# Query and key heads normed and rotated with tokens on partitions instead of features, in a two-block f32 kernel on one core

## What is computed

```python
def rms_norm(x, g):
    y = xf * lax.rsqrt(jnp.mean(xf * xf, axis=-1, keepdims=True) + EPS)
    return (y * g.astype(jnp.float32)).astype(x.dtype)

def apply_axial_rope(x, cos, sin):            # features as (2, 2, 32)
    xs = x.reshape(x.shape[:3] + (2, 2, HEAD_DIM // 4))
    x1, x2 = xs[..., 0, :], xs[..., 1, :]
    out = jnp.stack([x1 * c - x2 * s, x2 * c + x1 * s], axis=-2)
    return out.reshape(x.shape)
...
    bg_l, cg_l, vc_l, q_l, k_l, v_l, gt_l = jnp.split(hx @ w_in[layer], SPLITS, axis=-1)
    y_conv_l = conv_branch(bg_l, cg_l, vc_l, conv_w[layer])
    q = rms_norm(q.reshape(B, L, N_Q_HEADS, HEAD_DIM), q_g)   # split_heads
    k = rms_norm(k.reshape(B, L, N_KV_HEADS, HEAD_DIM), k_g)
    q_l = apply_axial_rope(q_l, cos, sin)
    k_l = apply_axial_rope(k_l, cos, sin)
    k_all = jnp.concatenate([k_c, k_l], axis=1)
    o_l = latent_attention(q_l, k_all, v_all)
```

## Time and profile before

| what | value |
|---|---|
| median of 3 runs | 1324.51 us (1324.28 to 1335.15) |
| the profiled execution, its own time | 1324.45 us |
| its span in the profile | 1322.6 us |
| PE busy | 1304.7 us, 99% of the span |
| DVE, ACT, POOL busy | 903.0 us (68%), 644.3 us (49%), 27.3 us (2%) |
| instructions | 23508 |
| HBM read | 227.63 MB |
| granted TensorE clock | full in all of the 40 slices |

### The profile page before, as it was taken

The page is one execution under the profiler, slowest core; times in us unless marked ns, Lnnn a source line. Parts: engine busy times, 40 slices in busy tenths (PEclk is TensorE's granted clock), DMA queues, the critical chain, the costliest instruction groups (busy, mean ns, idle before and its releaser), DMA issues. The chain is left out here.

```text
span 1322.6 us, 23508 instructions
## 1 busy us (share of the span) xinstructions
PE 1304.7 (99%) x9348; PEld 1210.0 (91%) x9348; DVE 903.0 (68%) x1455; ACT 644.3 (49%) x1027; POOL 27.3 (2%) x27
## 2 busy tenths in 40 slices
PE   9999999999999999999999999999999999999998
PEld 6788888888889999999999999989999999999998
DVE  4768775555658587554775555788887665689873
ACT  4622311222236345554555445666665765556552
POOL 0000000000010000000000000200000000100000
PEclk9999999999999999999999999999999999999999
DMA  9755555646635354545556665556546455436760
GB/s 358 270 186 191 191 191 192 222 159 215 204 107 161 111 159 130 159 128 160 178 155 194 190 201 174 171 159 184 148 143 181 128 174 176 145 112 208 217 197 33
DMA packets 201485, 230.20 MB, mean 174 GB/s; under 512 B 7073, under 2 KB 191649, under 8 KB 201377
## 3 DMA queue, kind: packets, MB, share of 16 engines
q1 hardware_dynamic: 201088, 228.42, 54.7%
q10 hardware_dynamic: 288, 0.28, 0.1%
HBM read 227.63 MB, written 1.05 MB: 173 GB/s over the span
## 5 line engine op out<-in xcount | busy, mean ns | idle before, releaser
L1105 PE MATMUL P<-XHB,WH 128*128 128x256 f32 (+1 forms) x1808 | 553.1, 306 | 7.4 <-DVE XLB L1784 3.9
L1106 PE MATMUL P<-XLB,WH 128*128 128x256 f32 (+1 forms) x1808 | 543.2, 300 | 0.0
L1107 PE MATMUL P<-XHB,WL 128*128 128x256 f32 (+1 forms) x1808 | 543.2, 300 | 0.0
L1988 DVE TENSOR_TENSOR WL<-W,WH 128x1024 fp32r<-128x1024 f32 x358 | 431.7, 1224 | 87.2 <-ACT WH L1565 87.0
L1565 ACT ACTIVATE WH<-W 128x1024 fp32r<-128x1024 f32 x358 | 369.0, 1042 | 249.3 <-PE P L1107 157.8
L1105 PEld LDWEIGHTS P<-XHB,WH 128*128 128x128 f32 x1808 | 340.0, 188 | 27.7 <-issue 8.2
L1106 PEld LDWEIGHTS P<-XLB,WH 128*128 128x128 f32 x1808 | 340.1, 188 | 15.2 <-issue 0.5
L1107 PEld LDWEIGHTS P<-XHB,WL 128*128 128x128 f32 x1808 | 340.2, 188 | 14.6
L1105 PE MATMUL P<-GH,WH 128*128 128x256 f32 (+1 forms) x372 | 121.2, 326 | 0.0
L1106 PE MATMUL P<-GL,WH 128*128 128x256 f32 (+1 forms) x372 | 120.6, 324 | 0.0
L1107 PE MATMUL P<-GH,WL 128*128 128x256 f32 (+1 forms) x372 | 120.6, 324 | 0.0
(11 more groups left out here) (322 smaller groups left out, 1797.3 us busy)
## 6 DMA issues: line engine op xcount, KB each, us to landing
W<-in_ffn_w_in SPq DMA_DIRECT2D x88, 512.0 KB, 4.8
W<-in_w_in_ab SPq DMA_DIRECT2D x72, 512.0 KB, 4.6
W<-in_w_modt SPq DMA_DIRECT2D x56, 512.0 KB, 3.9
W<-in_w_in SPq DMA_DIRECT2D x52, 512.0 KB, 4.1
W<-in_ffn_w_out SPq DMA_DIRECT2D x40, 512.0 KB, 4.8
W<-in_w_in_c SPq DMA_DIRECT2D x32, 512.0 KB, 4.3
W<-in_w_out_ab SPq DMA_DIRECT2D x16, 512.0 KB, 4.4
W<-in_w_out_c SPq DMA_DIRECT2D x16, 512.0 KB, 4.7
```

The lines of the kernel that those rows point to most:

```text
L1105: pe.matmul(o, h[:, k, c], xh[:, kk, a:b], start=kk == 0, stop=False)
L1106: pe.matmul(o, h[:, k, c], xl[:, kk, a:b], start=False, stop=False)
L1107: mm = pe.matmul(o, l[:, k, c], xh[:, kk, a:b], start=False, stop=kk == gm.nk - 1)
L1988: dve.tensor_tensor(l, a, h.bitcast(F32), ALU.subtract).then_inc(S["wl"], 1)
```

## The change

Queries and keys are now produced with tokens on partitions: the q and k gemms run unturned. k is then 96 matmuls of 256 columns in place of 48 of 512, and `K` and `Q` first hold tokens by features. Its second chunk is walked tile by tile. The unit of work of `qk_norm` is one gemm: two heads of q for 256 tokens, that is four blocks of 128 tokens by 128 features (u = 0 to 3), or k with eight blocks (u = 4). Each unit has three kinds of steps:

- `qs` (ACT, lines 1619 and 1623): each block is squared with a running sum over its row (`accum_out`), and one root is taken over 128x4 or 128x8 values.
- `qr` (DVE): one reciprocal of the same small size (2142); per block a scalar-tensor-tensor with the sine table on the swapped halves (2156) and one with the cosine table (2162), each of which multiplies also by the token's root; two additions of 128x256 (2167). The context blocks of k take one scalar-tensor-tensor each, by the gain (2153).
- `qt`: four PE transposes of 128x128 (1201), into one bank, and one ACT copy of 128x512 back to `Q` or `K` (1628, 1632). k has two such steps. PE waits there for all of the unit's DVE work.

The tables hold gain times cosine and gain times sine. One new DVE step `qg` makes them, 4 products of 128x256 (2133), put before the last part of the first feed-forward (gemm m=4 of f0=12, whose end is near 375 us in the trace of before). A new DMA brings 256 KB of gains. The columns of `w_in` that belong to q and k are reordered on the host. The `HOT` memsets, `perm` and lines 1215, 1221 and 1226 are gone. `qk_norm` is started after every q gemm, not after every second.

Diff, cut to its core ("..." is left-out text):

```diff
         for i in range(4):
-            self.gemm("q", i, WIN, 0, 8, 3072 + 256 * i, LAT, first=i == 0)
+            self.gemm("q", i, WIN, 0, 8, 3072 + 256 * i, LAT, turned=False, first=i == 0)
...
-            if i % 2:
-                self.call(lambda i=i: self.back.append(self.qk_norm(i // 2)))
+            self.call(lambda i=i: self.back.append(self.qk_norm(i)))
         self.call(self.reach, "ctx")
-        self.gemm("k", 0, WIN, 0, 8, 4096, ALL, first=True)
+        self.gemm("k", 0, WIN, 0, 8, 4096, ALL, turned=False, first=True)
         self.gemm("v", 0, WIN, 0, 8, 4352, ALL, turned=False)
-        self.call(lambda: self.back.append(self.qk_norm(2)))
+        self.call(lambda: self.back.append(self.qk_norm(4)))
...
+                if n == 1 and f0 == 12 and m == 4:
+                    self.call(lambda: self.step("qg"))
...
-    def qk_norm(self, s):
-        self.step("qs", a=s)
-        for _ in range(2):
+    def qk_norm(self, u):
+        self.step("qs", a=u)
+        yield
+        self.step("qr", a=u)
+        yield
+        yield
+        for v in range(2 if u == 4 else 1):
+            b, f = self.bank(self.up("qn"))
+            self.step("qt", a=u, b=v, bank=b, free=f)
...
             yield
-        b, f = self.bank(self.up("qr"))
-        self.step("qa", a=s, bank=b, free=f)
-        for _ in range(3):
-            yield
...
+            sp.dma_start(GR, w["qkg"].partition_broadcast(128).rearrange("p o c -> p (o c)")).then_inc(SX[0], 16)
...
-                elif s.kind == "qa":
...
-                    for i in range(4):
-                        n = 4 * s.a + i
-                        pe.wait_ge(S["qs"], n + 1)
-                        pe.matmul(ps[:, 0:T], HOT[:, 3 - i:131 - i], SQ[...], ...).then_inc(S["qh"], 1)
-                elif s.kind == "qb":
...
-                    pe.matmul(ps[:, 0:T], con("sel", 128 * s.b, 128 * s.b + 128),
-                              rows_of(s.a), start=True, stop=True).then_inc(S["qb"], 1)
-                elif s.kind == "rope":
...
-                    pe.matmul(ps[:, 0:T], con("perm"), ap, start=True, stop=True).then_inc(S["rm"], 1)
+                elif s.kind == "qt":
+                    pe.wait_ge(SI[5], 16)
+                    n = 4 if s.a == 4 else 2
+                    pe.wait_ge(S["rd"], 2 * s.a + 2)
+                    for h in (s.b,) if n == 4 else (0, 1):
+                        for j in range(n):
+                            c = 128 * j if n == 4 else 256 * h + 128 * j
+                            mm = pe.transpose(ps[:, c:c + 128], place(s.a, j)[:, 128 * h:128 * h + 128], con("id"))
+                    mm.then_inc(S["rm"], 1)
                 elif s.kind == "score":
...
-                    pe.wait_ge(S["rd"], end["q", h])
-                    pe.wait_ge(S["rd"], end["k", h // 4, 1])
-                    pe.wait_ge(S["qn"], end["k", h // 4, 0])
+                    pe.wait_ge(S["qn"], max(end["q", h], end["k", h // 4]))
...
+                            act.activation(SQ[...], y[:, 128 * h:128 * h + 128],
+                                           ACT.Square, accum_out=RQ[:, n:n + 1]).then_inc(S["qs"], 1)
...
+                    act.activation(RQ[:, 4 * s.a:n], RQ[:, 4 * s.a:n], ACT.Sqrt, scale=1.0 / 128, bias=con("eps")) \
...
+                    dve.reciprocal(rq, rq).then_inc(S["dv"], 1)
...
+                            dve.scalar_tensor_tensor(p, y[:, ::-1, :], r, sn, ALU.mult, ALU.mult).then_inc(S["ro"], 1)
...
+                        dve.scalar_tensor_tensor(y, y, rq[...], GT[:, g, t:t + 128], ALU.mult, ALU.mult)...
...
+                        dve.tensor_tensor(p, p, y, ALU.add).then_inc(S["rd"], 1)
```

More of the change, by code:

```diff
@@ L37 @@
 _at = 0
-for _name, _n in (("id", 128), ("one", 128), ("eps", 1), ("ee", 1), ("gat", 2), ("cnt", 26), ("perm", 128),
+for _name, _n in (("id", 128), ("one", 128), ("eps", 1), ("ee", 1), ("gat", 2), ("cnt", 26),
                   ("tri", 128), ("m01", 128), ("nst", 128), ("nca", 128), ("sel", 512), ("cos", 256), ("sin", 256)):
@@ L770, in missing @@
             h = i // 2
-            return not {("q", h), ("k", h // 4, 0), ("k", h // 4, 1)} <= self.ready
+            return not {("q", h), ("k", h // 4)} <= self.ready
         def score(i):
@@ L985, in build_program, with raws, place @@
         WIDE = {"s2": 512, "s3": T, "s4": 512, "s5": T, "s6": T, "s7": T}
-        def rows_of(s):
-            return MC[:, 7, :] if s == 2 else RS[:, 1, T * s:T * s + T]
-        def head(s, i):
-            if s < 2:
-                return Q[:, 4 * s + i, :], vec("qg"), True, ("qe", 4 * s + i + 1)
-            c = T * (i % 2)
-            return K[:, i // 2, c:c + T], vec("kg"), c > 0, ("ke", i // 2 + 1)
+        def raws(u):
+            return [(j, Q[:, 2 * u + j, :]) for j in range(2)] if u < 4 else [(j, KT[:, j, :]) for j in range(4)]
+        def place(u, j):
+            return QY[:, j if u == 4 else 2 * (u % 2) + j, :]
         DG = TS[:, 5, :]
@@ L1077, in chunk @@
                 order = [(j, k) for j in range(len(gm.tiles)) for k in range(s.nk)]
-                if gm.first:
+                if gm.first and not (kind == "k" and s.k0):
                     order.sort(key=lambda o: o[1])
@@ L2164, in _ @@
                     own += 1
                     dve.wait_ge(S["dv"], own)
-                    dve.wait_ge(S["ro"], n)
-                    dve.tensor_tensor(ap, ap, tmp, ALU.add).then_inc(S["rd"], 1)
+                    dve.wait_ge(S["qi"], 1)
+                    if u >= 2:
+                        dve.wait_ge(S["rm"], 4 if u == 4 else u - 1)
+                    heads, g = [(j, h) for j in range(k) for h in range(2)], 2 * (u // 4)
+                    for j, h in heads:
+                        d, t = slice(128 * h, 128 * h + 128), 128 * (j % 2)
+                        r, y, p = rq[:, 2 * j + h:2 * j + h + 1], raws(u)[j][1][:, d], place(u, j)[:, d]
+                        if j < k - 2:
+                            dve.scalar_tensor_tensor(p, y, r, GR[:, 256:384], ALU.mult, ALU.mult).then_inc(S["ro"], 1)
+                        else:
+                            p, y, sn = (v.rearrange("p (e c) -> p e c", e=2) for v in (p, y, GT[:, g + 1, t:t + 128]))
+                            dve.scalar_tensor_tensor(p, y[:, ::-1, :], r, sn, ALU.mult, ALU.mult).then_inc(S["ro"], 1)
@@ new lines, in _ @@
+                    for j, h in heads[-4:]:
+                        d, t = slice(128 * h, 128 * h + 128), 128 * (j % 2)
+                        y = raws(u)[j][1][:, d]
+                        if h == 0:
+                            dve.wait_ge(S["ro"], 8 * u + 2 * k - 4 + 2 * (j % 2) + 2)
+                        dve.scalar_tensor_tensor(y, y, rq[:, 2 * j + h:2 * j + h + 1], GT[:, g, t:t + 128], ALU.mult,
+                                                 ALU.mult).then_inc(S["ro"], 1)
+                    for j in (k - 2, k - 1):
+                        y, p = raws(u)[j][1], place(u, j)
+                        dve.wait_ge(S["ro"], 8 * u + 2 * k + 2 * (j % 2) + 2)
+                        dve.tensor_tensor(p, p, y, ALU.add).then_inc(S["rd"], 1)
@@ L2349, in vectors @@
     put("psc", a["pool_scale_2"])
-    put("qg", a["q_norm_g"])
-    put("kg", a["k_norm_g"])
     s, e = VEC["c"]
```

123 lines of the change are left out of this document (52 added, 71 removed).

## The result

The changed kernel takes 1331.24 us in the median of 20 executions (1326.77 to 1342.92), the kernel before 1324.62 us in 20 beside them (1323.96 to 1336.43). The ratio is 1.0053, with a 95% interval of 1.0033 to 1.0073. The profiled execution of the changed kernel is its fastest: 1326.77 us, with a span of 1324.9. The forecast was 1327.8 (1318.5 to 1336.0). So there are two things to explain: why the profiled execution gains nothing from 12 us less PE work, and why the median lies 4.5 us above it.

What follows compares the result with a forecast made beforehand. PE, busy 99% of the span, was taken to bound the kernel. From 1324.45 us, 11.8 less PE work, 14.3 of waits and 0.85 for restarts after them gave 1327.8 us, range 1318.5 to 1336.

Steps and rivals of the forecast that it cites:

- the clock: Slower rival: PE's clock falls in the long wait ahead of k, 0 to 3 us, 1330.8 at most; chance 0.07.
- the pace: Rival: gemms switch between two matmul paces, up to 6 us through the attention's end, 1321 or 1334; chance 0.08.
- unit 2, ahead of k: PE reaches these transposes at 420.65, DVE ends the unit at 427.4: 6.8 us wait, the largest item.
- unit 3: Between k's two chunks, PE ends the first at 433.6 and DVE the unit at 436.2: 2.6 us wait.
- unit 4: Ahead of vc0, PE is there at 459.3 and DVE ends the unit at 462.8: 3.5 us wait.
- PE's work: 34 fp32 products removed (14.6 us), transposes added (2.7) and narrower k matmuls (0.1): 11.8 us less.
- The walk: Step-by-step timing of PE's waits for DVE's units 0 to 4 in the transposing steps: 14.3 us in all.
- a clock that falls behind q3 with a slow chunk of k: Sign of being wrong: the granted clock falls behind q3 and the k chunk is slow.
- time from outside 400 to 465 us: Sign of being wrong: the time comes from somewhere outside that stretch of the trace.
- The rival on the faster side: DVE's and ACT's order covers the waits, only PE's sum counts: 1312.7 us; chance of mostly covered 0.14.
- Small pieces as dear as wide ones: Slower rival: 128-column products take 0.395 us and squares 0.5, adding 7.6 us, 1335.4; chance 0.13.
- Costing nothing: Tables (1.7 us, where DVE waits 5.4), gains' load, POOL's memsets and ACT's copies back add no time.

Runs made afterwards that it cites:

- e1_again: The changed kernel run again with nothing altered: 1334.98 us median of 8, its profiled execution 1326.21 us.
- after: The first profile of the changed kernel, its fastest of 20 executions: 1326.77 us, against a median of 1331.24 us.
- e8_look_b: Second further profile of the changed kernel, nothing altered: 1338.75 us.
- e9: Changed kernel with only the context tokens' norm hurried ahead of k, not the units: 1328.98 us median of 10, ratio to before 0.9993.
- e2: Changed kernel with units 1 to 4 behind the start of k, three half chunks before their transposes: 1325.81 us median of 12, ratio 1.0007.
- e3: Changed kernel with 14 overwritten fp32 products filling PE's wait ahead of unit 2's transposes: 1331.88 us median of 10.
- e7_look_a: First further profile of the changed kernel, nothing altered: 1336.44 us.

## Why the prediction was right, and where it was off

The mechanism was right for the profiled execution: PE's own work falls, PE waits for units in the transposing steps, and the two are about equal. What lifts the median above it stood in the forecast only as two small rivals, the clock and the pace. Step by step, in the first profile:

| term | forecast | measured |
|---|---|---|
| DVE per product of 128 columns | 0.26 us | 0.26 |
| ACT per square with its sum | 0.38 us | 0.29 |
| four transposes, taken as in the earlier trace rows | 0.445 us | 0.45 to 0.47 |
| wait of unit 0 | 1.3 us | 1.21 |
| unit 1 | 0.1 us | 0 |
| unit 2, ahead of k | 6.8 us | 6.49 |
| unit 3 | 2.6 us | 0 (the slow clock took 2.2 in its place) |
| unit 4 | 3.5 us | 2.91 |
| the waits in all | 14.3 us | 10.6 |
| PE's work | 11.8 us less | 8.7 us less |
| profiled execution | 1327.8 us | 1326.77 |

- **The walk** held to 0.6 us at each place that the clock left alone. That the sum came within 1.1 us is in part luck: 3.7 us of waits fewer and 3.1 us of savings fewer cancel. Its largest fault was ACT's squares: I had added the reading of the sum to a full piece of 0.29, but the two together take 0.29. Unit 4 was ready 1.0 us earlier than planned, and unit 3 0.6 to 0.8 us in the profiles that show its wait.
- **Clock.** I had it as a rival of 7 in 100, worth 0 to 3 us, with the remark that unit 3's wait would absorb it. It happened in all four profiles of the changed kernel. In the first it was absorbed as I had said: k's first chunk took 7.8 instead of 5.6 us, and the wait behind it was gone. It was a part of the likeliest case, not a rival to it, and the prediction's own sign of being wrong, a clock that falls behind q3 with a slow chunk of k, was there. The reading from the end of the trace, 3.9 us from PE's stop to the fall, was one case: in the long waits of the five profiles that have them it came after 2.3 to 5.3 us, and at unit 4 after 2.0 us in two profiles. There no wait stands behind to absorb it, and it cost 1.6 and 2.7 us.
- **Pace.** This is the term that was mis-sized. I gave it 8 in 100 and up to 6 us in either direction, for the stage up to the end of the attention alone. (My reading that v in the earlier trace rows is of the quicker kind was also wrong: v's matmuls start 0.118 us apart. The walk's 11.35 us for v fits that.) In fact the profile before has the quicker pace in nearly all of the attention and in the long stretch of the second block, so the changed one could mostly lose. The executions of the changed kernel draw the slower pace in the attention (3.1 us), in the long stretch (6.8 us), or in both. This, with a fall of the clock behind unit 4 in some (1.6 or 2.7 us), places the median 4.5 us above the profile. All of it arises behind 460 us and the pace's part behind 470, and time from outside 400 to 465 us was one of the prediction's own signs of being wrong. The forecast of the median was right by a range that had room for it, not because this was seen: that was luck.
- **The rival on the faster side** (waits covered, 1312.7) did not occur, but the version with all units behind k shows that its sum was right: 1313.84 at best. What stood against it in the prediction, that the room on DVE is behind k, is what the version uses.
- **Small pieces as dear as wide ones** was wrong: 0.26 and not 0.395.
- **Costing nothing**: the tables, the gains' DMA and POOL. The starts of the splits are 0.16 us apart at 99 us, at 350 us and again at 369 and 402 us. Between, four splits from 353 to 357 us start 1.1 us later, behind one instruction of DVE that lasts 2.33 us where it lasted 1.28 before (at 351.72, line 2037), and the one behind the tables (line 2133, 365.85 to 368.29) starts 2.4 us later; the distance is back to 0.16 us each time, so no part of this is on the path.

Open is what sets the pace. Most of its changes come where something else than f32r matmuls of 256 columns stands between them or PE waits, but not all: in the first profile it went from 0.118 to 0.113 us where v (unturned) ends and the next gemm (turned) begins, with no other instruction and no wait between. The first rows of that place:

```profile
453.13 0.28 PE L1097 MATMUL P<-WH,XLB 128*128 128x256 f32 x1
453.25 0.29 PE L1089 MATMUL P<-XHB,WH 128*128 128x256 f32 x1
453.37 0.28 PE L1090 MATMUL P<-XLB,WH 128*128 128x256 f32 x1
```

With four transposes between, it mostly kept its value; one added wait did not change it. None of the runs could choose it.

## What to carry to other kernels

Work moved off the engine that bounds the kernel pays only if its result is ready when that engine comes: count, for each hand-over, what stands ahead of the last producer in its own list, and how many steps a planner puts in between in the worst place (here a loop that hurries everything to reach one flag). Such a change is worth trying a second time with the hand-overs spread behind the point where the helper engine has room: here the same instructions went from 0.5% slower to 0.4 to 0.8% faster. And where times fall in groups, compare profiles of executions of the same group before looking for a cause in the edit.

## What the runs showed of the hardware beyond the forecast

- f32r matmuls of 256 columns follow each other at 0.1132 or 0.1176 us (160 us over 1414 or 1361 matmuls) at the same granted clock. The value can hold for over a hundred microseconds and is not the same in each execution of one program: 1541 matmuls from 680 us on cost 6.8 us more in one execution of the unchanged kernel than in another.
- In a wait of 6.5 us the granted clock fell to 0.50 some 5.3 us after PE had stopped, and came back 5.6 us after it had started again. In the kernel with the wait added it fell after 2.3 us and came back 5.5 us after the restart; in e1_again, with the same wait of 6.5 us, it fell after 2.5 us and came back 2.8 us after the restart. The first two cost about 2.2 us (on k's first chunk) and 2.5 us. Waits of 2.7 to 2.9 us stand ahead of unit 4 in seven profiles: the clock did not fall in two of them (after and e1_again), it fell 2.0 us after PE had stopped and before it started again in two (e8_look_b and e9), and 0.5 to 1.0 us after PE had started again in three (e2, e3, e7_look_a). The Trainium skill (TensorE: Matmul & The Clock Gate, Part 1: The HAM clock gate) speaks of a fall after idleness, and for the rise of a point that varies from run to run; the falls inside the waits agree with the first, and the returns 2.8 to 5.6 us behind the restart with the second.
- Squares of 128 columns with `accum_out` start every 0.29 us on ACT, their reading included (403.10, 403.39, 403.68, 403.98); pieces of that width without one started every 0.29 us too in the kernel before.
